# Starting the fixed buffers, the arena, the weight slots and the halves of x at multiples of 256 bytes in place of 64

## The reference, cut to what matters

```python
# first block
h = rms_norm(x, attn_norm); proj = h @ w_in
o_a = dsa_attention(...)      # top-64 keys by an index score, T5 bias
o_b = hgrn2_mixer(...)        # gated linear recurrence, chunks of 64
o_c = mla_attention(...)      # latent attention with rope
mixed = g_a * (o_a @ w_up_a) + g_b * (o_b @ w_up_b) + g_c * (o_c @ w_up_c)
x = x + mixed @ w_out
h = rms_norm(x, ffn_norm)
x = x + (silu(h @ w_ffn_gate) * (h @ w_ffn_up)) @ w_ffn_down
x = rms_norm(x, final_norm)
# second block
x = x + 0.5 * swiglu(rms_norm(x), w1...)          # 1024 -> 2816 -> 1024
x = x + merged(forgetting_attention, stick_breaking_attention) @ w_out_2
x = x + 0.5 * swiglu(rms_norm(x), w2...)
x = x + sigmoid(rms_norm(x) @ w_ple_gate) * (p @ w_ple_proj)
```

## Time and profile before

| what | value |
|---|---|
| median of three runs | 1059.37 us |
| span of the profiled execution, first to last instruction | 1057.7 us |
| PE busy | 1047.9 us (99%), 8760 matmuls |
| PEld busy | 1020.3 us (96%), 8760 weight loads |
| DVE busy | 741.0 us (70%) |
| ACT busy | 579.6 us (55%) |
| POOL busy | 77.0 us (7%) |
| TensorE's granted clock | full throughout |
| DMA | 187.81 MB, 178 GB/s on average |

### The profile page before, as it was taken

The page is one execution under the profiler, slowest core; times in us unless marked ns, Lnnn a source line. Parts: engine busy times, 40 slices in busy tenths (PEclk is TensorE's granted clock), DMA queues, the critical chain, the costliest instruction groups (busy, mean ns, idle before and its releaser), DMA issues.

```text
span 1057.7 us, 22212 instructions
## 1 busy us (share of the span) xinstructions
PE 1047.9 (99%) x8760; PEld 1020.3 (96%) x8760; DVE 741.0 (70%) x1098; ACT 579.6 (55%) x880; POOL 77.0 (7%) x92
## 2 busy tenths in 40 slices
PE   9999999999999999999999999999999999999998
PEld 8899999999999999999999999898889999999998
DVE  6799988747876666657666677667986876665666
ACT  5456655576565544556544445455666664554553
POOL 0000000001310000111000001041001300000110
PEclk9999999999999999999999999999999999999999
DMA  6356433344556554555555456464335455554563
GB/s 235 129 173 217 162 123 120 120 160 170 190 181 217 190 186 146 198 204 190 205 196 194 148 193 217 173 207 162 137 120 199 171 191 196 198 203 146 195 222 120
DMA packets 32444, 187.81 MB, mean 178 GB/s; under 512 B 3832, under 2 KB 7552, under 8 KB 14720
## 3 DMA queue, kind: packets, MB, share of 16 engines
q1 hardware_dynamic: 31472, 185.58, 50.3%
q0 software_dynamic: 416, 1.06, 0.4%
q10 hardware_dynamic: 496, 0.33, 0.2%
HBM read 184.98 MB, written 1.06 MB: 176 GB/s over the span
## 4 chain that ended last, share of the span: by engine, by line
PE 87%; DVE 6%; ACT 1%; issue 1%; DVEq 0%; ACTq 0%
PE acc L681 83%; PE area_a L681 2%; PE area_t L681 2%; DVE wlo L1575 2%; DVE s_sum L2133 0%; ACT he L1179 0%; ACT whi L1179 0%; PE area_t L947 0%; ACT s_a L1179 0%; DVE mask L1780 0%; DVE st L1765 0%; DVE score L1805 0%; DVE s_z L2135 0%; DVE s_a L2131 0%; DVE s_z L2037 0%
## 5 line engine op out<-in xcount | busy, mean ns | idle before, releaser
L681 PE MATMUL acc<-hs,whi 128*128 128x256 f32 x3584 | 624.6, 279 | 2.9 <-DVE wlo L1575 2.7
L681 PEld LDWEIGHTS acc<-hs,whi 128*128 128x128 f32 x3584 | 541.9, 187 | 10.1 <-issue 7.1
L681 PE MATMUL acc<-hs,wlo 128*128 128x256 f32 x1792 | 496.8, 277 | 0.0
L1179 ACT ACTIVATE whi<-raw 128x1024 fp32r<-128x1024 f32 (+3 forms) x379 | 357.2, 978 | 162.8 <-PE acc L681 136.6
L1575 DVE TENSOR_TENSOR wlo<-raw,whi 128x1024 fp32r<-128x1024 f32 (+4 forms) x259 | 272.1, 1092 | 98.5 <-ACT whi L1179 97.4
L681 PEld LDWEIGHTS acc<-hs,wlo 128*128 128x128 f32 x1792 | 336.1, 188 | 0.2
L681 PE MATMUL acc<-hid,whi 128*128 128x256 f32 x1056 | 180.9, 277 | 0.2 <-DVE wlo L1575 0.2
L681 PEld LDWEIGHTS acc<-hid,whi 128*128 128x128 f32 x1056 | 159.2, 188 | 0.4 <-DVE wlo L1575 0.4
L681 PE MATMUL acc<-hid,wlo 128*128 128x256 f32 x528 | 146.0, 277 | 0.0
L1663 DVE TENSOR_TENSOR wlo<-raw,whi 128x1024 fp32r<-128x1024 f32 x120 | 141.2, 1219 | 4.3 <-ACT whi L1179 4.2
L1676 DVE TENSOR_TENSOR hbuf<-acc,sbuf 128x256 f32<-128x256 f32 x66 | 28.0, 425 | 115.4 <-PE acc L681 112.0
(11 more groups left out here) (316 smaller groups left out, 1029.2 us busy)
## 6 DMA issues: line engine op xcount, KB each, us to landing
raw<-in_w_gu SPq DMA_DIRECT2D x66, 1024.0 KB, 4.8
raw<-in_w_dn SPq DMA_DIRECT2D x48, 704.0 KB, 4.0
raw<-in_w_up SPq DMA_DIRECT2D x10, 1024.0 KB, 4.8
raw<-in_w_gates1b SPq DMA_DIRECT2D x8, 1024.0 KB, 4.7
raw<-in_w_out SPq DMA_DIRECT2D x8, 1024.0 KB, 4.8
raw<-in_w_qk SPq DMA_DIRECT2D x8, 1024.0 KB, 4.8
raw<-in_w_gates SPq DMA_DIRECT2D x8, 1024.0 KB, 4.8
raw<-in_w_projT_b SPq DMA_DIRECT2D x7, 1024.0 KB, 4.8
```

Of the source, the lines that this page charges most:

```text
L681: return nc.tensor.matmul(out, w, m, start=start, stop=stop, skip_group_check=True)
L1179: return nc.scalar.activation(out, in_, f, **kw)
```

## The change

The allocator `fixed` rounds its start and each buffer's size up to 256 bytes in place of 64, so that each fixed buffer and the arena behind them begin at a multiple of 256. `SLOT` goes from 2080 to 2112 float32, so that the distance of the two slots goes from 8320 to 8448 bytes, 33 times 256. `hs_off` is rounded up to 256. No instruction, shape, count or order is touched, nor are the offsets within the arena.

```diff
-SLOT = 4 * FVL
+SLOT = (4 * FVL + 63) // 64 * 64
...
-        top = [nc.sbuf_base + (-nc.sbuf_base) % 64]
+        top = [nc.sbuf_base + (-nc.sbuf_base) % 256]
...
-            top[0] += (4 * int(np.prod(shape)) + 63) // 64 * 64
+            top[0] += (4 * int(np.prod(shape)) + 255) // 256 * 256
...
-        hs_off = base + 4 * ARENA
+        hs_off = (base + 4 * ARENA + 255) // 256 * 256
```

## The result

The changed kernel takes 1097.72 us (median of 4 runs, 1097.61 to 1097.77), the kernel before 1059.49 us beside it. The ratio is 1.0359, with a 95% interval of 1.0347 to 1.0372. That is 38.2 us more, far outside the range of the forecast.

What follows compares the result with a forecast made beforehand. PE, busy 1047.9 of 1057.7 us, was taken to bound the kernel through the distance between matmuls. Five terms of 0 on the 1057.7 us span, with the median 1.7 us above it, gave 1059.4 us; range 1056.0 to 1061.5 us.

Steps and rivals of the forecast that it cites:

- the loads: Weight tiles landing 4.8 us after issue: a slightly shorter landing is worth nothing in the body of the kernel.
- both ends: First weight landing and last add and store: 0 each, with ends of 0.4 us and 0.2 us either way.
- the one on the moving operand: 256-column products on PE: residues 192 and 64 both show 113.3 ns, 64 also 117.9, so alignment is worth 0.
- The step on the stationary operand: Weight slots at 128 and 0 both take 5.44 us per tile, so moving slot 0 is worth 0, within 0.8 us.
- a bound for the moving operand from the nearest row: 256-column products on PE: the nearest row above is the slow rhythm, 4.5 ns more per matmul.
- the ends: Limits around the summed change of 0: -0.8 - 0.3 - 0.4 - 0.2 = -1.7 and +1.7 us.
- The first rival: All moving operands at 0 remove PE's slow rhythm: 10.2 us less, 1049.2 us or further; chance 0.05.
- The slower rival: One feed-forward (`w_gu`) loop stays in the slow rhythm, costing 4.1 us: 1063.5 us; chance 0.13.
- the sign of error: Two neighbouring `w_gu` tiles should keep 5.44 us each; a value below means the moving operand's residue matters.
- the account of its cost: PE's matmul starts: 2,257 slow distances, each 4.5 ns above the fast rhythm, cost 10.2 us in all.
- The guess at its cause: The state in which PE comes out of a short wait seems to pick the fast or slow rhythm.

Runs made afterwards that it cites:

- fourth experiment: The changed kernel with `hs` at 128 and the arena at 192 mod 256, weights at 0 in both slots: 1080.66 us, ratio 1.0204.

## Why the prediction was wrong

What bounds the kernel was read rightly: PE and the distance between its matmuls. ACT, DVE, the loads and both ends came out at 0 as said. The kernel with the old residues for the big products' operands shows that for all of them together.

The step that failed is the one on the moving operand: "If the residue mattered, 192 and 64 should differ, and one residue should not give both. I take 0." It treats a residue as something that an operand has by itself. What counts is the offset between the moving operand and the weights, and of that the kernel before holds just two values, 64 and 192, spread alike over both slots. One residue gave both paces because offset 192 allows both. The step on the stationary operand has the same fault: slots at 128 and 0 put `hs` 64 and 192 away, and the two tiles showed one pace because PE carried its rhythm from the one to the other, and not because the offsets are alike. Kept throughout, 64 gives 117.8 ns and 192 gives 113.3 or 117.8. "The kernel before already holds all four residues, so its own trace is the experiment" was false for pairs. The change made a pair that no row of that trace holds, both at the same residue, and it costs 6.7 ns on every matmul.

A second fault is in the sum. The text has a bound for the moving operand from the nearest row, 4.5 ns more, and then leaves it out of the ends, which hold only 0.2 ns for the weights and nothing for the moving operand. Carried through for the 5,597 fast matmuls it gives 25 us, and a range up to some 1085 us. That would still have missed by 13 us, since the new pace is beyond both that the trace shows.

The first rival, "the residue sets the rhythm", had the mechanism in part and the sign wrong: it supposed that aligned is best. The slower rival had the sign, but for one loop kept at 117.8 ns; what came was 120.0 everywhere. What I listed as the sign of error, a tile of a `w_gu` loop off 5.44 us, is what the profile shows, on the other side.

The Trainium skill, "TensorE: Matmul & The Clock Gate", section "Part 2: What happens when you issue a matmul", says that TensorE has two independent read ports and that loading the next weights takes no bandwidth from the running matmul. The runs here differ with the placement of exactly these two operands: with the weights alone moved by 64 bytes, a tile went from 120.0 ns per matmul to 113.3 or 117.7. So for float32 operands of 128 and 256 columns the pace does depend on how the two operands lie to each other. Whether it is bandwidth that the weight load takes, or something else between the two, no run here shows.

On the rhythm, the account of its cost was right: 1,990 fewer slow distances took 9.0 us off PE's busy time, which fell by 10.0. The guess at its cause was half right. PE mostly keeps a rhythm until something at a border changes it, but which rhythms exist depends on the offsets, and in the kernel before the step from a tile at 64 to one at 192 goes with the switch to the fast one, without a stop.

What stays open: I didn't find why offsets of 0 and 96 are slow (that the reads of the two operands collide is a guess), nor why 192 has two rhythms and why 128 bytes more on `wlo` remove the slower one. Whether it is the load of a matmul's own weights that counts or that of the next one's wasn't separated. Only weights as stationary operand in 128 columns and a moving one of 256 columns were studied.

## What to carry to other kernels

When TensorE is the bound and each matmul has its own weight load, the start of the moving operand relative to the weights, mod 256 bytes, is a parameter like a tile size: try a few placements, and look at the distance between starts of matmuls in a steady loop. Rounding every buffer up to the same large alignment was as bad as any placement tried here. And when a trace is used as a natural experiment for a layout, ask which pairs of addresses it holds, not which addresses.

## What the runs showed of the hardware

The float32 matmul of 256 columns with its own weight load of 128 columns has a mean pace that depends on the offset: 113.3 ns at best, 117.0 to 119.9 at most offsets, 120.0 at 0. It is an even pace at 0 and a repeating pattern of unequal distances at 96. At an offset of 192 two paces exist, 113.3 and 117.8 ns. All nine `w_gu` loops at offset 192, of 960 matmuls each, kept one of them to the end; a `w_dn1` loop (fourth experiment) changed midway. With 192 throughout, runs of one and the same kernel spread: 1063.4 to 1068.4 us, against 1097.61 to 1097.77 for the kernel after, which has one pace. A pace passes from tile to tile: where tiles at 64 and 192 take turns, those at 64 can run at 113.3 ns, which they hardly reach alone.
